# Two arrays of split weight parts are allocated at a multiple of 2048 bytes of a partition

## What is computed

```python
def swiglu(h, wg, wu, wd):
    return (jax.nn.silu(h @ wg) * (h @ wu)) @ wd

for layer in range(DEPTH):                                  # DEPTH = 2
    h = h + hybrid_mixer(rms_norm(h, attn_norm[layer]), positions, layer, w_in[layer], ..., w_out[layer])
    hn = rms_norm(h, ffn_norm[layer])
    if layer % 2 == 0:
        h = h + swiglu(hn, dense_w_gate[j], dense_w_up[j], dense_w_down[j])      # 1024 x 3584 x 3
    else:
        h = h + moe_ffn(hn, moe_router[j], moe_w_gate[j], moe_w_up[j], moe_w_down[j])   # 8 of the same, top 2
return rms_norm(h, final_norm)
```

## Time and profile before

| | |
|---|---|
| time, 3 runs | 1554.97 us median (1553.34 to 1555.94) |
| profiled execution: time | 1553.95 us |
| its span in the trace | 1552.0 us |
| TensorE busy | 1513.9 us (98%) |
| VectorE busy | 1263.5 us (81%) |
| ScalarE busy | 1032.7 us (67%) |
| GpSimd busy | 73.0 us (5%) |
| mean granted TensorE clock | 0.985 of full |

### The profile page before, as it was taken

The page is one execution under the profiler, slowest core; times in us unless marked ns, Lnnn a source line. Parts: engine busy times, 40 slices in busy tenths (PEclk is TensorE's granted clock), DMA queues, the critical chain, the costliest instruction groups (busy, mean ns, idle before and its releaser), DMA issues.

```text
span 1552.0 us, 18927 instructions
## 1 busy us (share of the span) xinstructions
PE 1513.9 (98%) x7146; PEld 1250.1 (81%) x7146; DVE 1263.5 (81%) x1564; ACT 1032.7 (67%) x1332; POOL 73.0 (5%) x148
## 2 busy tenths in 40 slices
PE   8999999999998999999999999999999999999996
PEld 7877788887887788888888888888888888888885
DVE  6587655555558798999899999899899899999995
ACT  6454544443355367887787787787788788788784
POOL 4220000000213100000000000000000000000000
PEclk9979999999998899999999999999999999999999
DMA  8511645554343149999999999999999999999992
GB/s 291 197 56 55 229 170 186 193 177 159 122 144 109 56 163 375 378 365 375 352 353 366 353 359 372 349 359 373 355 359 372 346 368 352 371 373 365 363 371 93
DMA packets 181821, 431.61 MB, mean 278 GB/s; under 512 B 3808, under 2 KB 10336, under 8 KB 181728
## 3 DMA queue, kind: packets, MB, share of 16 engines
q1 hardware_dynamic: 180720, 428.01, 75.8%
q10 hardware_dynamic: 1008, 2.36, 0.4%
HBM read 429.31 MB, written 1.05 MB: 277 GB/s over the span
## 4 chain that ended last, share of the span: by engine, by line
PE 90%; DVE 6%; issue 1%; ACT 1%; POOL 1%; DMA 0%; DVEq 0%; SPq 0%; POOLq 0%; ACTq 0%
PE pair L864 50%; PE work L864 31%; PE work L836 2%; PE pair L930 2%; PE pair L836 2%; PE work L851 1%; PE work L1108 1%; PE work L1005 1%; DVE w_lo L1509 1%; DVE nmax L1599 1%; DVE arena L1585 0%; PE work L1122 0%; DVE arena L1568 0%; PE work L1123 0%; DMA h<-in_x 0%
## 5 line engine op out<-in xcount | busy, mean ns | idle before, releaser
L1509 DVE TENSOR_TENSOR w_lo<-ring,w_hi 128x1024 fp32r<-128x1024 f32 (+3 forms) x810 | 963.9, 1215 | 197.0 <-ACT w_hi L1207 183.2
L1207 ACT ACTIVATE w_hi<-ring 128x1024 fp32r<-128x1024 f32 (+3 forms) x810 | 840.1, 1053 | 321.5 <-PE pair L864 156.8
L864 PE MATMUL pair<-w_hi,hnT_hi 128*128 128x512 f32 x672 | 267.6, 398 | 2.4 <-DVE hnT_lo L1517 1.5
L864 PE MATMUL pair<-w_hi,hnT_lo 128*128 128x512 f32 x672 | 263.8, 393 | 0.0
L864 PE MATMUL pair<-w_lo,hnT_hi 128*128 128x512 f32 x672 | 261.2, 389 | 0.0
L864 PE MATMUL work<-w_hi,hidT_hi 128*128 128x512 f32 x552 | 217.8, 395 | 2.6 <-DVE hidT_lo L1760 1.4
L864 PE MATMUL work<-w_hi,hidT_lo 128*128 128x512 f32 x552 | 216.5, 392 | 0.0
L864 PE MATMUL work<-w_lo,hidT_hi 128*128 128x512 f32 x552 | 214.5, 389 | 0.0
L864 PE MATMUL pair<-w_hi,xU_hi 128*128 128x512 f32 x448 | 178.7, 399 | 0.0
L864 PE MATMUL pair<-w_hi,xU_lo 128*128 128x512 f32 x448 | 175.8, 392 | 0.0
L864 PE MATMUL pair<-w_lo,xU_hi 128*128 128x512 f32 x448 | 173.9, 388 | 0.0
(11 more groups left out here) (214 smaller groups left out, 1371.2 us busy)
## 6 DMA issues: line engine op xcount, KB each, us to landing
ring<-in_moe_w_gate SPq DMA_DIRECT2D x56, 2048.0 KB, 9.6
ring<-in_moe_w_up SPq DMA_DIRECT2D x56, 2048.0 KB, 9.7
ring<-in_moe_w_down SPq DMA_DIRECT2D x56, 2048.0 KB, 9.2
ring<-in_dense_w_gate SPq DMA_DIRECT2D x7, 2048.0 KB, 7.8
ring<-in_dense_w_up SPq DMA_DIRECT2D x7, 2048.0 KB, 7.8
ring<-in_dense_w_down SPq DMA_DIRECT2D x7, 2048.0 KB, 7.9
ring<-in_w_in SPq DMA_DIRECT2D x4, 2048.0 KB, 9.0
ring<-in_w_out SPq DMA_DIRECT2D x4, 2048.0 KB, 9.9
```

The source lines that it names most:

```text
L864: mm = pe.matmul(b, lhs[x_part][k + kk], w[w_part][:, kk, :], start=(first and kk == 0 and i == 0), stop=(last and kk == 1 and i == 2))
L1207: return act.activation(o, i, ACT.Copy)
L1509: dve.tensor_tensor(lo, raw, hi.bitcast(F32), ALU.subtract).then_inc(lo_done, 1)
```

## The change

The calls that allocate `layer_gains`, `cos`, `w_hi`, `w_lo` and `sin` now come first, in this order. `layer_gains` and `cos` fill the 1920 bytes up to offset 18432, which is 9 x 2048, and `w_lo` follows `w_hi` at another multiple. `sin` is placed so that all that follows is moved by 59392 bytes, 29 x 2048, and keeps its remainder. The three small tables get other remainders (in the list above). No instruction is added, removed or moved on any engine; each names the same buffers, shapes and waits, and only addresses differ.

```diff
         def sb(name, shape, dt=F32):
             return ctx.enter_context(nc.sbuf_tensor(name, shape, dt))
 
+        layer_gains = sb("layer_gains", [P, CQ + CKV + 2 * DB])
+        cos = sb("cos", [P, T, NF])
+        w_hi = sb("w_hi", [P, PARTS, 1024], F32R)
+        w_lo = sb("w_lo", [P, PARTS, 1024], F32R)
+        sin = sb("sin", [P, T, NF])
+
         with nc.sbuf_tensor("arena", [P, ARENA], F32) as arena:
             pass
 
@@ -219,9 +225,6 @@
         neg_chunk = sb("neg_chunk", [P, CHUNK])
         mask_q = sb("mask_q", [P, P], BF16)
         mask_k = sb("mask_k", [P, 2 * CHUNK], BF16)
-        cos = sb("cos", [P, T, NF])
-        sin = sb("sin", [P, T, NF])
-        layer_gains = sb("layer_gains", [P, CQ + CKV + 2 * DB])
         cgain, sgain = layer_gains[:, 0:CQ + CKV], layer_gains[:, CQ + CKV:]
         stat = sb("stat", [P, 2 * (2 * DEPTH + 1), 2])
         mhalf = sb("mhalf", [P, 4])
@@ -236,8 +239,6 @@
         rope_s = sb("rope_s", [P, HC * DR])
 
 
-        w_hi = sb("w_hi", [P, PARTS, 1024], F32R)
-        w_lo = sb("w_lo", [P, PARTS, 1024], F32R)
         used = [0]
```

## The result

The changed kernel takes 1574.84 us (median of 6 runs, 1573.15 to 1578.23) against 1555.45 us of the kernel before on the same chip: ratio 1.0107, 95% interval 1.0081 to 1.0134. By this ratio it is slower by 16.6 us, between 12.6 and 20.8; the two medians lie 19.4 us apart, inside that interval. The forecast was no change, 1555.0 us, with a range up to 1560 us.

The account below looks back on a forecast made before the run. The prediction took TensorE's matmul rate as the bound. Its four terms, 0 each, left the profiled execution's 1553.95 us, 1 us below the runs' median of 1554.97, so it forecast 1555.0 us, range 1543 to 1560 us.

Parts of the forecast that it names:

- a loss would show as 5.58 us for 24: Sign in TensorE's chain: 24 matmuls of 512 columns at L864 take 5.58 us instead of 5.49 to 5.50.
- (a): TensorE's moving reads of `w_hi` and `w_lo` at L864, remainder 1984 to 0: taken as 0, bounded by `pair_rows`.
- The last sentence of the prediction: It named as possible error a cost of streams of exactly one whole 2048-byte stretch, without a size.
- The slower rival: Streams at L864: the moving operand's remainder sets the rate, 3.5 ns more per matmul, 1573.8 us; chance 0.12.
- theory D: From the experiments, not the prediction: the streamed piece's distance from the stationary blocks, modulo 256 bytes, counts for matmul time.
- (b): ScalarE's write of `w_hi`, VectorE's read of it and write of `w_lo`: splits stay 1060 and 1223 ns, 0.
- (c): Move of everything to other absolute offsets, with `ring` keeping remainder and descriptors: taken as 0.
- (d): `cos`, `sin`, `layer_gains` at other remainders, read on GpSimd and VectorE: 0, some tenths of a us either way.
- "little faster" rival: 512-column matmuls at L864: crossing a multiple of 2048 costs 2.1 ns each, 11.3 us, giving 1543.7 us; chance 0.12.
- The rule of the Trainium skill: Matmul issue, N / 2.4 + 2.5 ns; as mechanism of the much faster rival, 1483.5 us, chance 0.02; not in the sum.

## Why the prediction was wrong

The bound was read rightly: TensorE's rate sets the end, and a shift of some ns in each of 5376 matmuls is how the addresses reached it. The line that a loss would show as 5.58 us for 24 came true.

The step that failed is (a), "I take 0, by the first row, the only one with both kinds side by side". The two kinds of `sel` piece, at remainders 896 and 1920, differ in whether they cross a multiple of 2048, and the row showed rightly that crossing costs nothing. But both lie at 128 modulo 256, like the blocks of `hn` that they meet. The pair varied the property that I had in mind and held the one that counts. It was a poor stand-in besides: where later runs moved `hn_low` out of phase, sixteen of these 256-column matmuls took 1.89 to 1.90 us, no more than the 1.92 before, so this row could hardly have shown the loss of the 512-column ones. The term measured 3.7 ns x 5376 = 19.9 us where the step had 0.

The same blindness ran through all comparisons: the kernel before had streams at a distance of 64 (`w`) or at 0 (`sel`, `y`, `extra`), and never at 128. The last sentence of the prediction looked for an unseen case, but named the wrong one, pieces that fill one whole stretch of 2048. The pieces at 1024 don't, and are as slow.

The slower rival had the amount, 1573.8 us, by luck, and not the mechanism. It took the 232.5 ns of `spread_result` as a property of remainder 128. With `w` at exactly that remainder the kernel ran at 1542.07 us, the fastest median of all (1544.68 when run again), and `spread_result` itself took 706.21 - 705.30 = 0.91 us for its four matmuls instead of 0.93, though neither `y` nor `selT` had another remainder:

```profile
705.30 0.23 PE work L1123
705.53 0.23 PE work L1124
705.75 0.23 PE work L1123
705.98 0.23 PE work L1124
706.21 3.85 PE pair L865 x17
```

This bounds theory D: `y` and `selT` are in phase with each other in every kernel, and still their matmuls followed the phase of `w`, also between one read of `y` and the next, where the trace's start times are 230.4 to 233.7 ns apart in the kernel before and 226.9 to 227.5 here. So a matmul's own distance does not settle its time alone. Why is open; that a slow stream ahead counts is in line with the run whose arrays lie apart, but wasn't tried by itself.

Steps (b), (c) and (d) held. The splits kept 1060 and 1224 ns; the absolute place cost nothing (ratio 1.0011 with the old remainder); the tables' moves cannot be told from nothing. What the kernel before had left to win by placement was real, too: 227 instead of 229 ns, some 2 ns x 5376 = 11 us. That is what the "little faster" rival had priced at 11.3 us, again for another reason, since the crossing costs nothing.

The rule of the Trainium skill that I weighed ("TensorE: Matmul & The Clock Gate", section "Back-to-back issue gap", 215.8 ns for 512 columns) stays unmet in every placement; the best is 226.7 ns. Of the 13 ns that the kernel before lies above it, placement returns 2; the other 11 stay unexplained. The same page, in "Step-by-step: what each phase is for", says that loading the next weights takes no read bandwidth from the running matmul. No run here measures bandwidth, but the two reads are not independent in time: 5.48 and 5.60 us stand side by side in one execution, with another stationary buffer and the same streamed arrays.

## What to carry to other kernels

Where TensorE's stream of matmuls is the bound, compare kernels by the distance between the start of the streamed operand and that of the stationary blocks modulo 256 bytes, and try 0 for all streams at once. This was shown for float32r matmuls of 512 columns with a weight load before each, not for other shapes: those of 256 columns did not slow down. From the worst to the best placement this kernel moves by 2 to 3%. A round address is worth nothing in itself. When near rows are to bound an unseen placement, write down every relation in which they agree, since a comparison is silent on what both of its sides share.

## What the hardware showed unexpectedly

- The distance from start to start of 512-column matmuls depends on two addresses together: 226.7 to 228.8 ns in phase, 229 ns at 64 bytes, 232 to 235 ns at 32, 128, 192 and 224. It is not monotone: 32 is worse than 64, and 64 differs from 192.
- The period is 256 bytes: 0 and 128 differ, while 256, between the streams (128 and 384) as well as from the blocks, is as good as 0. Absolute offset, a crossing of 2048 and the place of the ring made no difference.
- One of two alternating streams out of phase slows both (5.60 us for 24 where 5.49 were due), and matmuls that are in phase themselves (`spread_result`) take 0.93 us for four in the kernel before, whose `w` is out of phase, and 0.91 where `w` is in phase.
- That two reads meet in the same bank of the memory would explain a phase; no run looks into the memory, so it remains a guess.
